# State-space mixer of a two-block transformer: the third group's output projection moved behind the fourth group's tiles, and the decay subtraction moved one tile ahead with a third buffer

## The reference, cut to what matters

```python
def _ssd_chunked(xs, dt, a_neg, bm, cm):          # per group g: 8 heads, its own bm, cm
    def step(state, inp):                         # one chunk of 128 tokens
        xc, ac, bc, cc = inp
        acum = jnp.cumsum(ac, axis=1)
        seg = jnp.where(causal, acum[:, :, None] - acum[:, None, :], -jnp.inf)
        scores = jnp.einsum('btgn,bsgn->btsg', cc, bc)[..., None] * jnp.exp(seg)
        y_diag = jnp.einsum('btsgh,bsghp->btghp', scores, xc)
        y_off = jnp.einsum('btgn,bghpn->btghp', cc, state) * jnp.exp(acum)[..., None]
        w_end = jnp.exp(acum[:, -1:] - acum)
        new_state = (state * jnp.exp(acum[:, -1])[..., None, None]
                     + jnp.einsum('bsgn,bsghp->bghpn', bc, xc * w_end[..., None]))
        return new_state, y_diag + y_off

def _mamba2_mixer(h, in_w, conv_w, conv_b, dt_bias, a_log, d_skip, norm_g, out_w):
    z, xbc, dt = split(h @ in_w)
    xbc = silu(causal_dwconv(xbc, conv_w, conv_b))
    y = _ssd_chunked(...) + d_skip * xs
    y = y * silu(z)
    yg = rms_norm over each of the 4 groups of 512 features
    return (yg * norm_g) @ out_w
```

## Time and profile before

| | us |
|---|---|
| median of three runs (lowest, highest) | 3124.95 (3123.76, 3127.22) |
| the profiled execution | 3125.96 |
| its span | 3124.3 |
| PE busy in the span | 2945.9 |
| DVE busy | 1750.8 |
| ACT busy | 1009.9 |
| POOL busy | 414.3 |

### The profile page before, as it was taken

The page is one execution under the profiler, slowest core; times in us unless marked ns, Lnnn a source line. Parts: engine busy times, 40 slices in busy tenths (PEclk is TensorE's granted clock), DMA queues, the critical chain, the costliest instruction groups (busy, mean ns, idle before and its releaser), DMA issues.

```text
span 3124.3 us, 39886 instructions
## 1 busy us (share of the span) xinstructions
PE 2945.9 (94%) x16263; PEld 2297.6 (74%) x16263; DVE 1750.8 (56%) x1912; ACT 1009.9 (32%) x1309; POOL 414.3 (13%) x461
## 2 busy tenths in 40 slices
PE   2998999999999999999898999999979998999989
PEld 2885656667788888888777887878767886666667
DVE  5566726662455455543585747567454227676773
ACT  2123435551211111111233424234333114444452
POOL 0002000001011111100101112021101001332340
PEclk7998999999999999999899999999979999999999
DMA  6355011011133333321124223242311221212021
GB/s 229 108 169 132 4 28 29 8 28 41 48 115 120 115 101 111 116 76 47 36 65 128 80 83 107 68 135 75 107 56 37 98 88 61 68 35 68 35 74 61
DMA packets 245528, 249.16 MB, mean 80 GB/s; under 512 B 14021, under 2 KB 208418, under 8 KB 245378
## 3 DMA queue, kind: packets, MB, share of 16 engines
q1 hardware_dynamic: 221664, 170.39, 18.0%
q0 software_dynamic: 17680, 58.89, 6.3%
q10 hardware_dynamic: 6034, 17.74, 1.5%
HBM read 218.17 MB, written 26.45 MB: 78 GB/s over the span
## 4 chain that ended last, share of the span: by engine, by line
PE 79%; DVE 11%; issue 4%; ACT 4%; DMA 1%; ACTq 0%; SPq 0%; DVEq 0%
PE PU L973 16%; PE PU L975 16%; PE PU L974 16%; PE PM L1614 2%; PE PU L1592 2%; PE PU L1284 2%; DVE small L2757 2%; PE PM L1602 2%; PE PM L1634 2%; PE PM L1636 2%; PE PM L1635 2%; PE PU L987 2%; PE PU L1216 1%; PE PU L988 1%; PE PU L989 1%
## 5 line engine op out<-in xcount | busy, mean ns | idle before, releaser
L973 PE MATMUL PU<-hH,w_hi_t 128*128 128x512 f32 (+1 forms) x1872 | 739.1, 395 | 2.4 <-DVE w_lo_t L2349 2.4
L975 PE MATMUL PU<-hH,w_lo_t 128*128 128x512 f32 (+1 forms) x1872 | 730.7, 390 | 0.0
L974 PE MATMUL PU<-hL,w_hi_t 128*128 128x512 f32 (+1 forms) x1872 | 729.9, 390 | 0.0
L2349 DVE TENSOR_TENSOR w_lo_t<-w_raw,w_hi_t 128x1024 fp32r<-128x1024 f32 x181 | 228.6, 1263 | 357.4 <-ACT w_hi_t L1746 345.3
L973 PEld LDWEIGHTS PU<-hH,w_hi_t 128*128 128x128 f32 (+1 forms) x1872 | 351.4, 188 | 77.0 <-DVE w_lo_t L2349 3.8
L975 PEld LDWEIGHTS PU<-hH,w_lo_t 128*128 128x128 f32 (+1 forms) x1872 | 350.8, 187 | 76.0
L974 PEld LDWEIGHTS PU<-hL,w_hi_t 128*128 128x128 f32 (+1 forms) x1872 | 351.4, 188 | 72.2
L1746 ACT ACTIVATE w_hi_t<-w_raw 128x1024 fp32r<-128x1024 f32 x167 | 174.5, 1045 | 458.0 <-PE PU L975 356.3
L2825 DVE SCALAR_TENSOR_TENSOR xT<-PU,mod,xT 128x1024 f32<-128x1024 f32 x120 | 154.0, 1283 | 202.5 <-PE PU L975 202.5
L3106 DVE TENSOR_TENSOR_SCAN s_keep<-s_keep,zero 128x128 f32<-128x128 f32 (+7 forms) x128 | 180.6, 1411 | 2.0 <-POOL s_keep L928 2.0
L928 POOL TENSOR_SCALAR_AFFINE_SELECT s_keep<-s_keep 128x128 f32<-128x128 f32 x128 | 114.5, 910 | 501.5 <-ACT s_keep L2237 500.9
(11 more groups left out here) (419 smaller groups left out, 5003.8 us busy)
## 6 DMA issues: line engine op xcount, KB each, us to landing
ada_w<-in_ada_w_dram POOLq DMA_DIRECT2D x64, 384.0 KB, 4.0
w_raw<-in_w_gu_dram SPq DMA_DIRECT2D x44, 512.0 KB, 3.8
w_raw<-in_m_in_w_dram SPq DMA_DIRECT2D x40, 512.0 KB, 3.9
ada_w<-in_w_ada_dram POOLq DMA_DIRECT2D x32, 512.0 KB, 4.6
seg<-decay_sums SPq DMA_DIRECT2D x32, 512.0 KB, 4.7
w_raw<-in_w_down_dram SPq DMA_DIRECT2D x22, 512.0 KB, 3.4
w_raw<-in_w_in_dram SPq DMA_DIRECT2D x17, 512.0 KB, 3.9
ada_w<-in_w_ada_dram SPq DMA_DIRECT2D x16, 512.0 KB, 18.8
```

The costliest lines, as they stand in the source:

```text
L973: mm(PU[0:width, up, half, :], whi, aH[:, k, cols], start=k == 0, stop=False)
L974: mm(PU[0:width, up, half, :], whi, aL[:, k, cols], start=False, stop=False)
L975: last = mm(PU[0:width, up, half, :], wlo, aH[:, k, cols], start=False, stop=k == kt - 1)
L2349: V.tensor_tensor(w_lo_t[:, p, 0:w], w_raw[:, p, 0:w], w_hi_t[:, p, 0:w].bitcast(F32), ALU.subtract)\
```

## The change

- Group 2 is named `KEPT`. Its projection is no longer done ahead of group 3's tiles. SP stores `y_hi` and `y_lo` of group 2, 8 transfers of 512 KB, to DRAM (`scr_y`) as the tiles become ready; ACT, SP and POOL wait for all of these (`y_kept`) before they overwrite the memory in group 3.
- After the last z unit of group 3, SP loads the 8 tiles back into the first four tiles of `hH` and `hL`, which nobody reads then. PE does group 2's projection from there after its last tile, with group 3's 8 sums (in place of 64 instructions) and its spread put in after the fourth and fifth unit; then group 3's projection. DVE's scaling and its additions to `xT` are interleaved.
- Group 3 uses the same gating and squares as the other groups; POOL now adds its squares too.
- There are three decay blocks `seg[c % 3]`. `segments` (the subtraction alone) of tile c+1 stands on DVE ahead of `masked` of tile c, and on ACT `decays` of tile c+1 stands behind the z evacuation or the split of tile c. The `cbm` product moves from `segments` to `masked`.
- On SP the load of tile j+1's decays comes behind tile j's factors. From tile 2 on it therefore comes behind the wait for the output of tile j-2.
- Some semaphores are shared (`vec_done`, `stat_done`, `rp_landed`), with the same waits.

```diff
-        seg = at("seg", A + 11264, [P, 2, 8, P])
+        seg = [at(f"seg{n}", o, [P, 8, P]) for n, o in enumerate((A + 11264, A + 12288, A + 16384))]
 # SP
             def tile_decays(i, j):
+                if j >= 2:
+                    sp.wait_ge(bc_landed[j % 2], 16 * (4 * i + j // 2))
+                if j >= 3:
+                    sp.wait_ge(ss_y, TT * i + j - 2)
...
+                if i == KEPT + 1:
+                    for f in range(4):
+                        sp.wait_ge(y_lo_s, 4 * KEPT + f + 1)
+                        for part, tile in ((0, y_hi[KEPT]), (1, y_lo)):
+                            sp.dma_start(scr_y[part][f, :, :], tile[:, f, :].bitcast(F32)).then_inc(y_kept, 16)
...
                 for j in range(TT):
-                    if j >= 2:
-                        sp.wait_ge(ss_y, TT * i + j - 1)
-                    tile_decays(i, j)
-                    if j >= 2:
+                    if j < 2:
+                        tile_decays(i, j)
+                    else:
                         sp.wait_ge(ss_g, TT * i + j - 1)
                     tile_factors(i, j)
                     if j == 1:
                         z_panel(i, 3)
                     if j in (3, 5, 7) and i < NG - 1:
                         x_panel(i + 1, (j - 3) // 2)
                     if j in (3, 5) and i == NG - 1:
-                        out_panels(i, ((j - 3) // 2,))
-            out_panels(NG - 1, (2, 3))
+                        out_panels(KEPT, ((j - 3) // 2,))
+                    if 1 <= j < TT - 1:
+                        tile_decays(i, j + 1)
+            n = m_unit(NG - 1) + 6 + 3
+            sp.wait_ge(unit_done[n % 2], n // 2 + 1)
+            for f in range(4):
+                for part, tile in ((0, hH), (1, hL)):
+                    sp.dma_start(tile[:, f, :].bitcast(F32), scr_y[part][f, :, :]).then_inc(y_back[f // 2], 16)
+            out_panels(KEPT, (2, 3))
+            out_panels(NG - 1, range(4))
 # PE
-                if i:
+                if 0 < i <= KEPT:
                     group_out(i - 1)
...
-            group_sums(NG - 1)
-            group_spread(NG - 1)
+            group_out(KEPT, {3: lambda: group_sums(NG - 1), 4: lambda: group_spread(NG - 1)})
             group_out(NG - 1)
 # ACT
+                if i == KEPT + 1:
+                    act.wait_ge(y_kept, 16 * 8)
+                if not 0 < i <= KEPT:
+                    activate(i, 5)
+                decays(i, 0)
                 for c in range(TT):
...
-                    decays(i, c)
                     if c % 2 == 0:
                         split()
                     else:
                         p = unit()
-                        free(af(zf[:, c // 2, :], unit_ps(p), ACT.Silu if last else ACT.Copy))
+                        free(af(zf[:, c // 2, :], unit_ps(p), ACT.Copy))
+                    if c + 1 < TT:
+                        decays(i, c + 1)
 # DVE
             def segments(i, c):
                 b = c % 2
                 ve.wait_ge(bc_landed[b], 16 * (4 * i + c // 2 + 1))
-                V.tensor_tensor(seg[:, b, :, :], seg[:, b, :, :],
+                V.tensor_tensor(seg[c % 3][:, :, :], seg[c % 3][:, :, :],
                                 acum[:, c, 8 * i:8 * i + 8].unsqueeze(2).broadcast_to([P, 8, P]), ALU.subtract).then_inc(ss_seg, 1)
+
+            def masked(i, c):
                 ve.wait_ge(ss_cb, TT * i + c + 1)
                 if TT * i + c:
                     ve.wait_ge(ss_m, TT * i + c)
                 V.tensor_tensor(cbm[:, :], PM[:, 3, 0:P], tri[:, :], ALU.mult).then_inc(ss_cbr, 1)
-
-            def masked(i, c):
...
+                segments(i, 0)
                 for c in range(TT):
                     if c >= 2:
                         state_update(i, c - 2)
                         output(i, c - 2)
-                    segments(i, c)
                     if c % 2 == 0:
                         split()
                         skip()
+                    if c + 1 < TT:
+                        segments(i, c + 1)
                     masked(i, c)
```

More of the change, by code:

```diff
@@ L225, in two_blocks @@
     scr_g = nc.dram_tensor("mixer_inverse_rows", (KD, TT, 2, P), F32, kind="Internal").ap()
+    scr_y = [nc.dram_tensor(f"kept_group_{n}", (4, P, T), F32, kind="Internal").ap() for n in ("high", "low")]
     ctx = ExitStack()
@@ L879, in _ @@
                 g.wait_ge(cv_tok, 5 * i + 4)
-                if i:
+                if i == KEPT + 1:
+                    g.wait_ge(y_kept, 16 * 8)
+                elif i:
                     n = m_unit(i) + 6 + KD - 1
@@ L1226, in head_sums @@
                     last = mm(PM[:, 2 + n % 2, w * t:w * (t + 1)], u_sq[:, t * P:(t + 1) * P], sel, start=True, stop=True)
-                last.then_inc(c_sum, 1)
+                last.then_inc(stat_done, 1)
             c0 = cr()
@@ L1482, in ssd_out @@
                         last = mm(PM[hd * HD:(hd + 1) * HD, 0, f * P:(f + 1) * P], xdt[:, h * HD:(h + 1) * HD],
-                                  seg[:, c % 2, h, :], start=True, stop=True)
+                                  seg[c % 3][:, h, :], start=True, stop=True)
                 last.then_inc(ss_y, 1)
             def group_sums(i):
-                tiles = 1 if i < NG - 1 else 4
-                for f in range(tiles):
-                    if i < NG - 1:
-                        pe.wait_ge(m_add, 3 * (i + 1))
-                    else:
-                        pe.wait_ge(m_sq, 4 * i + f + 1)
-                    for t in range(TT):
-                        last = mm(PM[:, 2, t:t + 1], xt[:, t, f * P:(f + 1) * P], ones[:, 0:1],
-                                  start=f == 0 and t == 0, stop=f == tiles - 1 and t == TT - 1)
+                pe.wait_ge(m_add, 3 * (i + 1))
+                for t in range(TT):
+                    last = mm(PM[:, 2, t:t + 1], xt[:, t, 0:P], ones[:, 0:1], start=t == 0, stop=t == TT - 1)
                 last.then_inc(n_sum, 1)
@@ L1504, in group_spread, with group_out, ready @@
                 last.then_inc(c_bc, 1)
-            def group_out(i):
+            def group_out(i, after={}):
+                high, low = (hH, hL) if i == KEPT else (y_hi[i], y_lo)
+                def ready(k):
+                    if i == KEPT:
+                        pe.wait_ge(y_back[k // 2], 64)
+                    else:
+                        pe.wait_ge(y_lo_s, 4 * i + k + 1)
                 for c in range(4):
@@ L1509, in group_out @@
                     for u in range(2):
-                        ready = (lambda k: pe.wait_ge(y_lo_s, 4 * i + k + 1)) if c == u == 0 else None
-                        feat_unit(wp, u * P, P, 4, y_hi[i], y_lo, panel_last=u == 1, ready=ready)
+                        feat_unit(wp, u * P, P, 4, high, low, panel_last=u == 1, ready=ready if c == u == 0 else None)
+                        if 2 * c + u in after:
+                            after[2 * c + u]()
             assert uc.n == M_UNIT0 + 1, (uc.n, M_UNIT0)
@@ L2135, in group_root, with group_high @@
                 af(m_rt[:, :], PM[:, 2, 0:TT], ACT.Sqrt, bias=EPS, scale=1 / 512).then_inc(c_root, 1)
-            def group_high(i):
-                for f in range(4):
+            def group_high(i, tiles=range(4)):
+                for f in tiles:
                     act.wait_ge(m_sc, 4 * i + f + 1)
@@ L2174, in _ @@
                             activate(i, 5)
-                last = i == NG - 1
+                if i == KEPT + 1:
+                    act.wait_ge(y_kept, 16 * 8)
+                if not 0 < i <= KEPT:
+                    activate(i, 5)
+                decays(i, 0)
                 for c in range(TT):
-                    if c == 0 and i == 0:
-                        activate(i, 5)
-                    decays(i, c)
                     if c % 2 == 0:
@@ L2818, in low, with evacuated @@
                 V.tensor_tensor(f_lo[:, t, :], f_prod[:, t, :], f_hi[:, t, :].bitcast(F32), ALU.subtract).then_inc(f_act, 1)
+            def evacuated(g, t):
+                p = unit()
+                free(V.scalar_tensor_tensor(xT[:, t, :], unit_ps(p), m(g, t), xT[:, t, :], ALU.mult, ALU.add))
             def down_units(g, tiles):
@@ L2823, in down_units @@
                 for t in tiles:
-                    p = unit()
-                    free(V.scalar_tensor_tensor(xT[:, t, :], unit_ps(p), m(g, t), xT[:, t, :], ALU.mult, ALU.add))
+                    evacuated(g, t)
             def ffn_body(i, times, jobs):
@@ L2976, in gated @@
                     V.tensor_tensor(z3, z3, xt[:, :, f * P:(f + 1) * P], ALU.mult).then_inc(m_gate, 1)
-            def last_gated(first, end, signal):
-                ve.wait_ge(ss_g, TT * (NG - 1) + end)
-                for f in range(4):
-                    n = m_unit(NG - 1) + 6 + KD + f
-                    ve.wait_ge(unit_free[n % 2], n // 2 + 1)
-                    z3 = zf[:, f, first * P:end * P].rearrange("p (t c) -> p t c", c=P)
-                    ins = V.tensor_tensor(z3, z3, xt[:, first:end, f * P:(f + 1) * P], ALU.mult)
```

(8 more changed lines are left out.)

61 lines of the change are left out of this document (34 added, 27 removed).

## The result

| | before | changed |
|---|---|---|
| median, us (lowest, highest; four runs each) | 3124.36 (3118.93, 3127.22) | 3205.29 (3203.74, 3206.69) |
| ratio, with its 95% interval | 1 | 1.0261 (1.0243, 1.0279) |
| span of the profiled execution, us | 3124.3 | 3205.1 |
| clock granted to TensorE, mean | 0.972 | 0.963 |
| PE busy, us | 2945.9 | 2954.7 |

The changed kernel is 2.6% slower; 3205 had been forecast. PE does the same products and is busy only 9 us longer, so the rest of the 81 us is idle. The page of the changed kernel names it: first the busy times, then the chain that ended last by engine, then the group of DVE's subtraction.

A forecast was written before the change was run, and what follows sets the result against it. PE was taken to bound the tile loops; loops +57.6, starts +19.6, output 7 -2 and group 3 with tail +4.7 summed to +80 us on 3124.95, forecasting 3205 us, range 3165 to 3245.

The forecast's parts named there:

- What bounds it: Tile loops: PE bounds the kernel before, at 8.69 us per tile, 52.1 us for six tiles.
- the tail as the place where the change pays: After group 3's last output: 74.7 us at PEclk 0.79, some 31 us of it wait, sums, spread and half clock.
- wins 17.6: Tail: said to win 17.6 us, with slower loops and late scores taking more than all, leaving +4.7.
- part 2: Group starts: scores 1 wait for a later `cbm` 0; +9.2 us each for groups 1 to 3, +1.2 in group 0.
- Part 1: DVE's subtraction waits for a load queued behind factors and the preceding output; tiles take 12.7 and 14.2 us against PE's 8.7.
- The sum per group, 74.5 us: Output 0 to output 6 in each group: 72.0 us plus 2.5 for lower clock in the last tile.
- How PE waits: Tile loops: PE idles 4 to 6 us for `cbm` in each tile, outputs 12.7 and 14.2 us apart by turns.
- Half clock, the rival: Loops: array stays at 1.2 GHz, 14.5 to 15.3 us per tile, 3253 us in all; 13%.
- The term of 2.5 us for each long wait: PE's half unit behind a long idle runs partly at the lower clock, costing 2.5 us.
- Part 3: SP's store of group 2: eight transfers in 13.6 us, landed before `cT`; costs 0 us.
- the load-back: Tail: loads take 13.6 us, end 10.5 after output 6; rival at half rate, projection 14 later, 3219 us, 8%.
- Output 7: Groups 0 to 2: PE's wait for tile 6's output, up to 0.9 us each, goes; -2 us.

The follow-up runs named there:

- run 6: Changed kernel with the decay part undone (two buffers, old order), leaving only the held-back projection; 3106.59 us, ratio 0.9938 to the kernel before.
- Run 1: Changed kernel with SP's load of the next tile's decays ahead of its wait for output j-2, from tile 2 on; 3119.28 us, ratio 0.9979.
- Run 3: Changed kernel with only tile 0's causal product moved back directly behind its subtraction, loads still late; 3199.39 us, ratio 1.0237.
- run 5: Changed kernel with decay loads ahead of the wait, tile 2's load ahead of the z panel's, tile 0's causal product early; 3097.57 us, ratio 0.9919.
- run 2: Changed kernel with the decays' load behind the wait for output j-2 but ahead of factors and weight panel; 3145.76 us, ratio 1.0069.
- run 7: Kernel before with only the decay part added: three blocks and the new order on SP, DVE and ACT; 3222.67 us, ratio 1.0304.

## Why the prediction was right

- **What bounds it, and the tail as the place where the change pays: right.** The dense tail ran at full clock, and the held-back projection alone gave -19 us. The prediction's "wins 17.6" is no forecast of that run: it is group 3 and the tail with six tiles at PE's pace (52.1) and with part 2's 9.2 in it already, so the sentence counts part 2 twice (the sum of the forecast does not). Its terms for holding back alone are -37.6 and +18.1, that is -19.5. That this is so near the 19 measured is partly luck: run 6 has -5.4 and +2.5 for group 3's loop and start that this prediction did not have, and its tail is 2.4 us longer than forecast.
- **Part 1, a load behind its own trigger: right, and shown.** Run 1 moves the load and nothing else, and 86 us go. The periods alternate on DVE as forecast, 12.7 and 14.2 us: 14.2, 12.6, 15.2, 12.5 in group 0, and 14.1 to 14.4 and 13.1 to 13.7 in the others. DVE stood 154.5 us in all, against some 130. The sum per group, 74.5 us, was measured as 75.1, 75.8, 73.9 and 75.3. Of its pieces the landings were 0.3 us shorter than forecast: a median of 4.5 for tiles 3, 5 and 7 (4.8) and of 5.5 for tiles 4 and 6 (5.8). The rest of the period was longer by about as much; seen are subtractions of 1.5 to 2.1 us in place of 1.2 in six of the 32 tiles, and `masked` of 1.7 us in eight.
- **How PE waits: wrong in shape, right in sum.** I had 4 to 6 us in front of each scores product and outputs on PE 12.7 and 14.2 apart. The long and short waits alternate instead: scores 4 to 7 of group 0 waited 5.9, 1.1, 6.5 and 1.5, and PE's outputs 3, 4 and 5 end 9.8 and 17.5 apart. Behind a wait of 6 us the way from scores to output took 10.0 us, behind 1.1 us it took 7.6. So the lower clock uses up 2.3 us of the idle time in one tile, which shortens the next wait; the rest of the difference is DVE's own alternation of longer and shorter periods. DVE's chain is the bound and doesn't notice.
- **Half clock, the rival: refuted as a bound.** A stretch's mean of 0.88 to 0.91 is not 0.5. The term of 2.5 us for each long wait was about right (2.3).
- **Part 2, the late `cbm`: the size was right for this kernel, the independence was not.** Starts of groups 1 and 2 grew by 9.5 and 9.2 us (forecast 9.2), with waits of 7.07 and 6.71 (6.7). But the text prices it as a cost of its own. Run 3 takes it away and gets 6 us, not 29: behind it stands tile 2's late block, and the loop behind both starts at DVE's `output` 0. Only with the loads early too (run 1 to run 5, 3119.28 to 3097.57) is it worth most of its price, 22 of 29 us; run 5 also moves tile 2's load, and how the 22 divide between the two was not tried. In group 0 it costs 2.0 (forecast 1.2).
- **Part 3, the store, and the load-back: right.** The eight stores took 14.1 us (13.6) and had landed at 2242.4, 17 us ahead of scores 0; the eight loads back took 13.4 (13.6). PE waited 0.80 us for the last of them, with the products of the first two tiles done, as forecast. Scores 0 of group 3 came 81.5 us after output 6 of group 2 (81.9). Group 2's projection started 8.3 us after output 6 (forecast "in effect" 9.1) and both projections with sums and spread took 92.1 (93.5). These two make the 2.3 us by which the tail is shorter than forecast.
- **Output 7: half right.** I had PE's wait for tile 6's `output` ahead of it go, for -2 in groups 0 to 2. Output 6 to output 7 went from 8.0 to 7.6 us, a third of a microsecond for each group. In group 3 the wait is 4.5 us, and I had not named it. It costs little, since the last tile came back from DRAM only at 2368.3, and PE had to wait for that anyway.
- **The number itself: luck in its last digit.** 3205 was forecast and 3205.29 measured, but the lines of the account are off by up to 2.3 us and partly cancel (81.3 against 80.0), and what lies outside the account gives another -0.6.

For the landing I had weighed a rule of the Trainium skill, DMA: Bandwidth & Descriptors, section "Anatomy of one DMA", by which I estimated 3.2 us for 512 KB. The section gives its fit for transfers that GpSimd issues, and these are issued by SP, so the estimate goes beyond what the page states. In these runs blocks landed in 3.3 us at the fastest, a median of 3.7 for tiles 3 to 7 where no transfer of SP's stood just in front (run 2), 4.5 behind the factors and 5.5 behind a panel as well. No run was below the estimate, but most were 0.5 to 2.3 us above it, and the measurement decides.

## What to carry to other kernels

When an instruction is moved a step ahead, everything that feeds it has to move too: look for the load's place in its queue, and for the semaphore in front of it, because in this kernel the third buffer and the earlier subtraction cost 97 us while the load waited for the same event that its consumer follows (run 7), and gained some 9 once it did not. Costs at two places of one chain don't add: take away the one at the loop's pacer first (here 86 us), after which the other is worth most of its price (22 us of 29, and only 6 before). Judge the result by the periods of the pacing engine, since the waits of the engine behind it may alternate with the clock.

## What the runs showed of the hardware that was not expected

- A 512 KB broadcast load (tiles 3 to 7) landed in a median of 3.7 us when it was issued ahead of the three factor transfers (run 2), in 4.5 when behind them and in 5.5 when behind a weight panel too (the changed kernel). The three factor transfers carry 512 KB in all (2 x 128 and 256 KB) and were issued over 1.9 us.
- In the changed kernel's loops PE falls into a pattern of two tiles (scores 4 to 7): a wait of 5.4 to 6.5 us with a half unit that runs in part at the lower clock, then a wait of 1.1 to 2.8 us. Behind these short waits the half unit ran at full clock six times of eight; ahead of scores 7 of groups 1 and 3 waits of 2.82 and 2.47 us had a slower one (PEclk 0.83 and 0.84), while other waits of 2.47 us had not. The way from scores to output was 7.6 us at full clock and 10.0 behind the wait of 5.9.
- PE's two projections in 92 us, with DVE, ACT and POOL at work and two of the eight loads back still landing at their start, ran at PEclk 1.00. The tail before, with waits in it, had 0.79.
